# A sorted MoE tail on one core: the second tile's gathers and both bias loads moved behind the last expert's silu, the first gate product moved ahead of the last down product, and the sample rows taken third instead of fourth

## The reference

```python
h = h + hier_moe(rmsnorm(h))                 # 32 experts, gate/up 1024x256, down 256x1024, two experts a row
gate = sigmoid(rmsnorm(h, norm_ple) @ ple_gate_w + ple_gate_b)     # ple_gate_w is 1024x1024
h = h + gate * (p @ ple_proj_w)
y = rmsnorm(h, norm_final)
```

## Time and profile before

| | before |
|---|---|
| time, median of 3 runs (lowest to highest) | 545.56 us (544.63 to 545.68) |
| the profiled execution: its own time | 543.69 us |
| the profiled execution: its span | 541.5 us |
| mean granted TensorE clock in it | 0.979 of full |
| PE busy | 505.9 us (93%) |
| DVE, ACT, POOL busy | 218.3, 155.9, 125.9 us |
| DMA moved | 154.16 MB, mean 285 GB/s |

### The profile page before, as it was taken

The page is one execution under the profiler, slowest core; times in us unless marked ns, Lnnn a source line. Parts: engine busy times, 40 slices in busy tenths (PEclk is TensorE's granted clock), DMA queues, the critical chain, the costliest instruction groups (busy, mean ns, idle before and its releaser), DMA issues.

```text
span 541.5 us, 7999 instructions
## 1 busy us (share of the span) xinstructions
PE 505.9 (93%) x3140; PEld 307.6 (57%) x3140; DVE 218.3 (40%) x542; ACT 155.9 (29%) x322; POOL 125.9 (23%) x191
## 2 busy tenths in 40 slices
PE   5999999999999998899999999999999784999992
PEld 4888886788545555455555554545555342444451
DVE  2187696523034457664322221121122212367565
ACT  1436263122615021112222231222322211433242
POOL 0300059994201002101123110110123130222121
PEclk9999999999999999899999999999999977999997
DMA  8993000944469924999999999999999999940011
GB/s 304 398 323 117 1 1 21 377 147 94 155 264 396 418 88 177 370 400 412 418 411 412 417 419 415 417 419 411 421 412 419 414 418 416 375 145 40 39 41 41
DMA packets 42441, 154.16 MB, mean 285 GB/s; under 512 B 14524, under 2 KB 15164, under 8 KB 33220
## 3 DMA queue, kind: packets, MB, share of 16 engines
q1 hardware_dynamic: 32900, 130.26, 61.1%
q0 software_dynamic: 6640, 17.62, 8.6%
q10 hardware_dynamic: 2864, 5.77, 2.9%
HBM read 146.02 MB, written 21.53 MB: 309 GB/s over the span
## 4 chain that ended last, share of the span: by engine, by line
PE 78%; DMA 11%; DVE 6%; ACT 2%; SPq 1%; issue 1%; POOL 0%; ACTq 0%; POOLq 0%; DVEq 0%
PE PS L1112 16%; PE PS L877 10%; PE PS L683 10%; DMA mem<-in_exp_w_up 9%; PE PS L1221 9%; PE PS L1133 9%; PE PS L643 5%; PE PS L654 5%; PE PS L1023 3%; DMA mem<-in_w_a 2%; DVE mem L1911 1%; PE PS L941 1%; PE PS L1119 1%; PE PS L991 1%; PE PS L826 1%
## 5 line engine op out<-in xcount | busy, mean ns | idle before, releaser
L1112 PE MATMUL PS<-mem 128*64 128x256 f32 x512 | 121.7, 392 | 12.8 <-DMA mem<-in_exp_w_up 12.6
L1113 PE MATMUL PS<-mem 128*64 128x256 f32 x512 | 121.7, 392 | 0.0
L1112 PEld LDWEIGHTS PS<-mem 128*64 128x64 f32 x512 | 69.4, 141 | 56.0 <-DMA mem<-in_exp_w_up 13.1
L683 PE MATMUL PS<-mem 128*128 128x260 f32 x320 | 73.3, 385 | 0.0
L1113 PEld LDWEIGHTS PS<-mem 128*64 128x64 f32 x512 | 69.4, 141 | 0.0
L2263 DVE TENSOR_TENSOR mem<-PS,mem 64x256 f32<-64x256 f32 x32 | 13.7, 427 | 133.7 <-ACT mem L1461 133.7
L683 PEld LDWEIGHTS PS<-mem 128*128 128x128 f32 x320 | 59.8, 190 | 10.5 <-issue 1.5
L1133 PE MATMUL PS<-mem 128*64 128x512 f32 x256 | 61.9, 604 | 0.8 <-DVE mem L2266 0.8
L877 PE MATMUL PS<-mem 128*128 128x512 f32 x128 | 56.6, 596 | 0.0
L1221 PE MATMUL PS<-mem 128*128 128x512 f32 (+1 forms) x144 | 56.3, 547 | 0.0
L1461 ACT ACTIVATE mem<-PS 64x256 f32<-64x256 f32 x32 | 12.1, 377 | 116.3 <-PE PS L1113 116.3
(11 more groups left out here) (334 smaller groups left out, 583.4 us busy)
## 6 DMA issues: line engine op xcount, KB each, us to landing
mem<-in_exp_w_down SPq DMA_DIRECT2D x32, 1024.0 KB, 22.1
mem<-in_exp_w_gate SPq DMA_DIRECT2D x32, 1024.0 KB, 18.0
mem<-in_exp_w_up SPq DMA_DIRECT2D x32, 1024.0 KB, 20.7
mem<-in_w_out SPq DMA_DIRECT2D x2, 2048.0 KB, 13.2
mem<-in_ple_gate_w SPq DMA_DIRECT2D x2, 2048.0 KB, 37.8
mem<-in_x_prompt SPq DMA_DIRECT2D x4, 512.0 KB, 14.6
mem<-in_w_v SPq DMA_DIRECT2D x1, 2048.0 KB, 24.8
mem<-in_w_z SPq DMA_DIRECT2D x1, 2048.0 KB, 29.4
```

The lines of the kernel that those rows point to most:

```text
L683: ins = pe.matmul(PS[b + h][:, 0:HALF], w[:, k, :], aT[:, k, h * HALF:(h + 1) * HALF], start=(k == 0), stop=(k == KT - 1))
L1112: pe.matmul(PS[0][0:S, 0:FF], rows_k, gu[slot][:, k, :], start=(k == 0), stop=(k == KT - 1))
L1113: ins = pe.matmul(PS[1][S:2 * S, 0:FF], rows_k, gu[slot][:, KT + k, :], start=(k == 0), stop=(k == KT - 1))
```

## The change

Nothing is computed otherwise; only orders change, on all five engines, and two PSUM bank numbers with them.

- POOL: `gather_h` and `gather_choices` of the second tile, and `gather_h` of tile 2, go behind the third scatter.
- ACT: the two bias loads go behind the last silu (and change places); the fourth `take_y` goes behind the squares of the first two positions.
- PE: `gates(0, 0)` goes ahead of `end_down(3)`, and `h2_rows(1)` behind `gates(0, 1)`.
- `TAIL`: samples third, tile 2 fourth.

```diff
-TAIL = [0, 1, 2, 4, 3]
+TAIL = [0, 1, 4, 2, 3]
...
-GATE_BANKS = [(0, 1), (2, 3), (0, 1), (2, 2), (3, 4, 5)]
+GATE_BANKS = [(0, 1), (2, 3), (4, 4), (0, 1), (2, 3, 5)]
...
             end_act_rows(3)
+            gates(0, 0)
             end_down(3)
-            gates(0, 0)
+            gates(0, 1)
             h2_rows(1)
-            gates(0, 1)
             pe.wait_ge(s_pp_out, len(PP_UNITS))
             gates(1, 0)
             h2_rows(2)
             gates(1, 1)
             h2_rows(3)
+            pe.wait_ge(s_ysb_free, n * U + (HEAD + LAST))
+            gate_samples(2)
             pe.wait_ge(s_f_gb, 2)
-            gates(2, 0)
+            gates(3, 0)
             h2_rows(4)
-            gates(2, 1)
+            gates(3, 1)
             pe.wait_ge(s_f_gb, 4)
-            gate_samples(3)
-            pe.wait_ge(s_ysb_free, n * U + (HEAD + LAST))
...
             end_silu(1)
-            act.dma_start(bfin, a["norm_final"].unsqueeze(0).to_broadcast((P, D))).then_inc(ld_bias, 16)
-            act.dma_start(bple, a["ple_gate_b"].to_broadcast((P, D))).then_inc(ld_bias, 16)
             end_take_y(0)
             end_silu(2)
             end_take_y(1)
             end_silu(3)
+            act.dma_start(bple, a["ple_gate_b"].to_broadcast((P, D))).then_inc(ld_bias, 16)
+            act.dma_start(bfin, a["norm_final"].unsqueeze(0).to_broadcast((P, D))).then_inc(ld_bias, 16)
             end_take_y(2)
-            end_take_y(3)
             A(ss[:, 20:21], eps, ACT.Sigmoid)
             norm_h2(0)
             norm_h2(1)
+            end_take_y(3)
...
-            for t in range(2):
-                gather_h(t)
+            gather_h(0)
             end_scatter(1)
             for q in range(2):
                 pool.wait_ge(y_written[q], n * 16 + 16 * (HP // 2))
                 idle_step(n * 12 + (6 + q))
-            for t in range(2):
-                gather_choices(t)
+            gather_choices(0)
+            end_scatter(2)
+            gather_h(1)
+            gather_choices(1)
             pool.wait_ge(s_up_done, n * U + (HEAD + 2))
-            idle_step(n * 12 + 8)
+            idle_step(n * 12 + 9)
             gather_h(2)
-            end_scatter(2)
+            root_h2(0)
             pool.wait_ge(y_written[0], n * 16 + 16 * (HP // 2 + 1))
             idle_step(n * 12 + 10)
             gather_choices(2)
+            root_h2(1)
             end_scatter(3)
-            root_h2(0)
-            root_h2(1)
             gather_h(3)
...
             combine(1)
+            dve.wait_ge(ld_bias, 32)
+            gate_sum(0, 0)
             take_h2_rows(1)
-            dve.wait_ge(ld_bias, 32)
+            gate_sum(0, 1)
             dve.wait_ge(s_pp_out, len(PP_UNITS))
-            gate_sum(0, 0)
-            combine(2)
-            gate_sum(0, 1)
             apply_gate(0, 0)
             apply_gate(0, 1)
-            take_h2_rows(2)
             finish(0)
+            combine(2)
             combine(3)
```

More of the change, by code:

```diff
@@ L35 @@
 PP_FIRST = 12
-GATE_BANKS = [(0, 1), (2, 3), (0, 1), (2, 2), (3, 4, 5)]
-ROOTS = [(2, 0), (2, 1), (2, 2), (3, 0), (2, 3), (2, 4), (3, 1), (3, 2), (3, 3), (3, 4)]
+GATE_BANKS = [(0, 1), (2, 3), (4, 4), (0, 1), (2, 3, 5)]
+ROOTS = [(2, 0), (2, 1), (3, 0), (2, 2), (2, 3), (3, 1), (2, 4), (3, 2), (3, 3), (3, 4)]
 EMPTY = 4096
@@ L632, in _ @@
             sp.dma_start(Yg[4][0:NS], y_dram[2 * SEQ:2 * TOK, :].rearrange("(p k) n -> p k n", k=2)).then_inc(yg_full[4], 16)
-            sp.wait_ge(s_f_y, NT - 1)
+            sp.wait_ge(s_f_y, 3)
             sp.dma_start(o["y_s"][:, 0, :], yout[4][0:NS, :]).then_inc(st_fin, 16)
@@ L1567, in _ @@
             norm_h2(1)
+            end_take_y(3)
             sigmoid(0, 0)
-            norm_h2(2)
             sigmoid(0, 1)
@@ L1572, in _ @@
             square_h3(0, 1)
+            norm_h2(2)
             norm_h2(3)
-            norm_h2(4)
             sigmoid(1, 0)
@@ L1578, in _ @@
             square_h3(1, 1)
+            norm_h2(4)
             sigmoid(2, 0)
             sigmoid(2, 1)
+            sigmoid(3, 0)
             square_h3(2, 0)
             square_h3(2, 1)
-            sigmoid(3, 0)
             sigmoid(3, 1)
-            sigmoid(4, 0)
             square_h3(3, 0)
             square_h3(3, 1)
+            sigmoid(4, 0)
             sigmoid(4, 1)
@@ L1744, in _ @@
             idle_step(n * 12 + 3)
-            END_IDLE = [4, 5, 9, 11]
+            END_IDLE = [4, 5, 8, 11]
             def end_scatter(q):
@@ L1803, in _ @@
             gather_choices(3)
-            root_h2(2)
             root_h3(0)
             store_sorted(0)
+            root_h2(2)
             root_h2(3)
-            root_h2(4)
             root_h3(1)
             store_sorted(1)
+            root_h2(4)
             root_h3(2)
-            store_sorted(2)
             root_h3(3)
+            store_sorted(3)
             root_h3(4)
@@ L2377, in _ @@
             combine(1)
+            dve.wait_ge(ld_bias, 32)
+            gate_sum(0, 0)
             take_h2_rows(1)
-            dve.wait_ge(ld_bias, 32)
+            gate_sum(0, 1)
             dve.wait_ge(s_pp_out, len(PP_UNITS))
-            gate_sum(0, 0)
-            combine(2)
-            gate_sum(0, 1)
             apply_gate(0, 0)
             apply_gate(0, 1)
-            take_h2_rows(2)
             finish(0)
+            combine(2)
             combine(3)
             gate_sum(1, 0)
-            combine(4)
+            take_h2_rows(2)
+            gate_sum(1, 1)
             take_h2_rows(3)
-            gate_sum(1, 1)
             apply_gate(1, 0)
             apply_gate(1, 1)
+            combine(4)
             gate_sum(2, 0)
+            gate_sum(2, 1)
             finish(1)
             take_h2_rows(4)
-            gate_sum(2, 1)
             apply_gate(2, 0)
@@ L2401, in _ @@
             gate_sum(3, 0)
+            finish(2)
             gate_sum(3, 1)
-            finish(2)
             apply_gate(3, 0)
@@ L2406, in _ @@
             gate_sum(4, 0)
+            apply_gate(4, 0)
             finish(3)
-            apply_gate(4, 0)
             t = TAIL[NT - 1]
```

## The result

| kernel | median us (lowest to highest) | ratio to before, 95% interval | profiled: own time, span, mean clock |
|---|---|---|---|
| before | 545.59 (544.63 to 545.68) | | 543.69, 541.5, 0.979 |
| changed | 555.23 (551.98 to 555.97) | 1.0166 [1.0129, 1.0202] | 551.98, 549.8, 0.975 |
| changed, timed again beside `down_ahead` and `busy_wait` | 555.38 (550.00 to 558.89) | 1.0160 [1.0108, 1.0213] | 554.96, 552.8, 0.967 |

The account below looks back on a forecast made before the run. Bound by the weight stream until some 457 us, PE's own work after 468, then the last tile's norm and store. Seven terms summed to +6.6 us: 550.3 profiled, 552.2 as median; range 547.3 to 555.3.

Parts of the forecast that it names:

- rival 4: Pairs of tile 2 also get ahead of half 0 of w_ple, both clock losses full: +9.8, 555.4 us; chance 0.13.
- Start of the first gate product: gates(0, 0) starts at 467.7 instead of 468.49, as half 0 of w_ple lands at 467.6: -0.8 us (-2.6 to +1.2).
- Down product: The last down product runs between gates(0, 0) and gates(0, 1), no longer while PE would wait: +1.9 us.
- Transposes next to their reader: With h_rows(1) transposes directly ahead of gates(1, 0), PE waits for DVE to take the first half: +0.3 us (0 to 0.6).
- Samples: Samples third: PE waits at h2_rows(2) for their combine, behind finish(0) in DVE's list: +2.9 us (2 to 3.5).
- Clock ahead of the first gate product: PE idles 7.4 us, then gates(0, 0) runs at half clock with only PE behind: +2.2 us (1.6 to 3.4).
- Clock behind the samples' stall: The stall of nearly 3 us at the samples can bring half clock again: +1.0 us (0 to 1.7).
- The end: apply_gate(4, 0) comes ahead of the samples' finish(3), so the last gate_sum follows PE's end at once: -0.9 us.
- Rival 1: Moved transfers give way to the weights, gates(0, 0) starts at 460.3 without clock loss: -4.0, 541.6 us; chance 0.08.
- Rivals 2 and 3: 2: half 0 near 465.9, warm PE, 547.5 to 548.6 us, chance 0.17; 3: nothing measurable, no samples' stall, 545.6, chance 0.04.

Follow-up runs that it names:

- down_ahead: Changed kernel with the last down product ahead of gates(0, 0) again, transfers and all else as changed: 551.27 us, ratio 1.0105 to before.
- busy_wait: Changed kernel with eight matmuls on constants, result unread, added in PE's idle time ahead of gates(0, 0): 550.01 us, ratio 1.0080 to before.
- changed_again: The changed kernel with nothing altered, timed again on one chip with other kernels beside it: 555.38 us, ratio 1.0160 to before.
- weights_first: Changed kernel with tile 1's gathers, tile 2's h rows and the bias loads held until half 0 of w_ple landed: 544.20 us, ratio 0.9963 to before.
- both: Changed kernel with the edits of weights_first and samples_first together: 543.61 us, ratio 0.9974 to before.
- old_order_weights_first: Kernel before, its PE and DVE orders and TAIL kept, with the moved transfers held until half 0 of w_ple landed: 540.40 us, ratio 0.9920.
- bias_late: Changed kernel with only the two bias loads held until half 0 of w_ple landed: 552.11 us (one execution).
- samples_first: Changed kernel with the samples' combine moved on DVE ahead of apply_gate(0, 0), from behind finish(0): 549.11 us, ratio 1.0060 to before.
- gathers_late: Changed kernel with only tile 1's gathers and tile 2's h rows held until half 0 of w_ple landed: 544.34 us (one execution).

## Why the prediction was right or wrong

Slower, 552.2 us forecast, 555.23 measured, inside the range (547.3 to 555.3) by 0.1 us. That it lies inside is luck: the second timing, 555.38, lies just outside. The narrower interval with the chance of 0.58, +5 to +8.3 us, was missed. The measured +9.6 is the figure of rival 4 (+9.8), of which half came true: both losses of clock, but not pairs of tile 2 ahead of half 0 (they were issued at 467.40, 2.4 us before it landed, and q0 moved 0.02 MB from 466 to 468 us). The direction and the mechanism of the main terms were right; the sum was 3 us short. By its terms, with the changed kernel's two profiles:

- *Start of the first gate product*, forecast -0.8: 469.87 - 1.34 = 468.53, so 0.0 in the first profile; in changed_again, 1.7 us late at the loop's last scatter, 469.58 is 0.6 before it. Right within its bounds. The up weights of the last expert landed 5.0 us earlier (PE began at 453.76, less 1.34, against 457.39), not 6.2, and it made no difference, as said.
- *Down product* +1.9: 1.87. *Transposes next to their reader* +0.3: 0.44 of wait.
- *Samples* +2.9: 1.38 + 1.03 = 2.41 of wait; the mechanism and the releasers are those forecast, down to `finish(0)` 1.84 us behind DVE's last operation.
- *Clock ahead of the first gate product* +2.2: 2.4 and 2.7. The wait was 7.42 us, forecast 7.4.
- *Clock behind the samples' stall*, taken as +1.0 between 0 and 1.7: the term that was mis-sized. It was 0 in the first profile and 2.8 in changed_again, and 1.7 to 2.8 in six of the eight profiles with this stall. The bound came from one row of before in which the half clock lasted 3.3 us; in weights_first and changed_again it lasted some 6.7 us.
- *The end* -0.9: PE ended at 519.35 + 20.66 = 540.01 and the span 9.8 later, against 10.65 before, -0.85.

From the start of the first gate product to PE's end it was 70.1 us against 62.4 before; the terms (2.4, 1.9, 0.4, 2.4) give 7.1 of these 7.8, and the rest is spread over the restarts of the transposes, 0.1 to 0.2 us each, which the sum left out. The first profile's span, less 1.34 us, is thus 7.0 us above before's; with changed_again's 2.8 us for the second loss that makes +9.8, about what the medians show (+9.6 and +9.8). Of the 3 us that the forecast was short, 1.8 are this term. I had hedged between nothing and a full loss and so named a value that neither execution had.

One reading of the earlier trace rows was off, without consequence for the sum: the DMA row is at 9 from the 17th slice on, not from the 24th.

Rival 1, that the moved transfers give way, is refuted by half 0's 36.3 us, and by the packets. The experiments turned it into a kernel, weights_first: the changed kernel's orders with transfers that are made to give way. Its first gate product starts at 460.36, where the rival said 460.3, but it takes 544.20 us and not 541.6: the rival had no loss of clock, and behind the samples' stall its profile has one of 2.8 us. Rivals 2 and 3 fall with the landing of half 0 (469.82, less 1.34, so 468.5 and not 465.9) and with the stall of 2.41 us. The fastest kernel, 540.40 us, is another one: it has the orders of before.

## What to carry to other kernels

A transfer that is moved behind a wait isn't moved behind the stream. In this saturated stretch half 0 landed when the bytes that the other queues got in before it were through, even those issued long after it (the bias rows at 459.2, half 0 at 433.6), and in 2 KB runs it got 20 to 22% of the bytes beside packets of 4 and 8 KB. Hold the other transfers on the landing that matters, not on a point in the program that happens to lie before it, and then look at who needs them: in `both` and in `old_order_weights_first` the held pairs were the next thing waited for.

When PE idles ahead of work that nothing hides, count the half clock behind the wait too. All six waits of 3.9 to 7.6 us ahead of the first gate product were followed by it, at a cost of 1.5 to 2.8 us that didn't grow with the wait (2.7 us behind 3.92 in bias_late, 1.6 behind 6.33 in samples_first). Behind the stall of 1.4 and 1.0 us it came in six of eight profiles, and behind waits of 1.81 us (gathers_late) and 2.18 us (`both`) it didn't come: there the forecast has to hold both cases. And before a short tile is moved forward, look at what the engine that feeds it has in its list.

## What I had not expected of the hardware

A stall of 1.38 + 1.03 us, with a transpose of 0.41 us in it, was followed by half clock in six of eight profiles, for some 6.7 us in weights_first, which made a 7.1 us product take 9.9. The same program did and didn't do it. The mean clocks fit that as a part of the changed kernel's spread: 0.973 in the execution of 550.00 us, 0.964 to 0.967 in those of 554.96 to 558.89 us of the same lot. How large a part isn't shown, as only two executions were profiled.
